# One layer of a streaming encoder on one core: the low parts of a weight panel made by GpSimd in four instructions instead of two

## What is computed

```python
proj = x @ w_in                                   # (T,1024) @ (1024,1792)
q, k = _partial_rotary(q), _partial_rotary(k)     # parts of proj
attn = window attention over chunks of 64         # 8 heads, 2 kv heads, with sinks
c_in = u[..., :512] * sigmoid(u[..., 512:])       # the rest of proj
c = silu(layer_norm(depthwise_conv31(c_in)))
mix = concatenate([attn, c]) @ w_out              # (T,1024) @ (1024,1024)
h = layer_norm(ALPHA * x + mix)
up = depthwise_conv3(h @ w_up)                    # (T,1024) @ (1024,5632)
f = (silu(up[..., :2816]) * up[..., 2816:]) @ w_down
ple = sigmoid(h @ w_pg + b_pg) * (p @ w_pe)
y = layer_norm(ALPHA * h + f + ple)
```

## Time and profile before

| | |
|---|---|
| median of three runs | 2382.76 us (2382.01 to 2384.76) |
| the profiled execution | 2384.01 us, span of its trace 2382.1 us |
| TensorE busy with matmuls | 2347.3 us, 99% |
| VectorE busy | 1423.9 us, 60% |
| ScalarE busy | 1134.5 us, 48% |
| GpSimd busy | 1364.3 us, 57% (1351.5 of it in L545) |
| granted TensorE clock, mean | 0.996 |

### The profile page before, as it was taken

One profiled execution on the slowest core, in us unless ns is written; L12 is line 12 of the kernel. 1 busy time (PEld: TensorE's weight loads), 2 busy tenths in 40 slices (PEclk: granted clock), 3 DMA queues, 4 the chain that ended last, 5 costly groups with the idle time before them and its releaser, 6 DMA issues.

```text
span 2382.1 us, 32873 instructions
## 1 busy us (share of the span) xinstructions
PE 2347.3 (99%) x12705; PEld 2183.0 (92%) x12705; DVE 1423.9 (60%) x2060; ACT 1134.5 (48%) x1859; POOL 1364.3 (57%) x1078
## 2 busy tenths in 40 slices
PE   8999999999999999999999999999999999999997
PEld 8889999999989899999989999999989999999996
DVE  7868777644767665426766765267666553663232
ACT  4446554443555443425554524246535243664452
POOL 7455566576644555557544554676555547676663
PEclk9999999999999999999999999999999999999998
DMA  6333333344333333353433332444333324354432
GB/s 203 111 119 103 125 115 120 118 152 150 108 124 108 104 107 101 115 164 108 136 104 98 106 114 90 143 146 153 98 98 106 114 90 154 118 167 135 143 113 86
DMA packets 99979, 289.77 MB, mean 122 GB/s; under 512 B 13425, under 2 KB 37105, under 8 KB 99825
## 3 DMA queue, kind: packets, MB, share of 16 engines
q1 hardware_dynamic: 82560, 261.77, 35.2%
q10 hardware_dynamic: 17264, 25.91, 3.3%
HBM read 278.74 MB, written 8.99 MB: 121 GB/s over the span
## 4 chain that ended last, share of the span: by engine, by line
PE 95%; DVE 3%; ACT 1%; POOL 0%; DMA 0%; issue 0%; DVEq 0%; ACTq 0%
PE ps L613 31%; PE ps L614 30%; PE ps L615 30%; PE ps L672 1%; PE ps L701 1%; PE ps L692 1%; PE ps L681 1%; DVE turned L1158 1%; DVE sq L1320 0%; DVE res L1257 0%; PE ps L734 0%; DVE turned L1155 0%; DMA a_raw<-in_xT 0%; DVE ps L1157 0%; PE ps L725 0%
## 5 line engine op out<-in xcount | busy, mean ns | idle before, releaser
L545 POOL TENSOR_TENSOR w_lo<-w_raw,w_hi 128x512 fp32r<-128x512 f32 (+2 forms) x1060 | 1351.5, 1300 | 978.3 <-ACT w_hi L772 972.4
L772 ACT CAST w_hi<-w_raw 128x1024 fp32r<-128x1024 f32 (+2 forms) x529 | 516.3, 981 | 552.7 <-PE ps L615 486.8
L613 PE MATMUL ps<-h_hi,w_hi 128*128 128x450 f32 (+5 forms) x2080 | 742.3, 357 | 0.2 <-DVE h_lo L1407 0.2
L614 PE MATMUL ps<-h_lo,w_hi 128*128 128x450 f32 (+5 forms) x2080 | 735.6, 354 | 0.0
L615 PE MATMUL ps<-h_hi,w_lo 128*128 128x450 f32 (+5 forms) x2080 | 734.7, 353 | 0.0
L613 PEld LDWEIGHTS ps<-h_hi,w_hi 128*128 128x128 f32 x2080 | 392.2, 189 | 30.8 <-issue 7.7
L614 PEld LDWEIGHTS ps<-h_lo,w_hi 128*128 128x128 f32 x2080 | 392.2, 189 | 22.1 <-issue 1.5
L615 PEld LDWEIGHTS ps<-h_hi,w_lo 128*128 128x128 f32 x2080 | 391.9, 188 | 21.0
L613 PE MATMUL ps<-f_hi,w_hi 128*128 128x448 f32 (+2 forms) x1072 | 383.1, 357 | 0.0
L614 PE MATMUL ps<-f_lo,w_hi 128*128 128x448 f32 (+2 forms) x1072 | 377.4, 352 | 0.0
L615 PE MATMUL ps<-f_hi,w_lo 128*128 128x448 f32 (+2 forms) x1072 | 377.4, 352 | 0.0
(11 more groups left out here) (153 smaller groups left out, 1935.4 us busy)
## 6 DMA issues: line engine op xcount, KB each, us to landing
w_raw<-in_panels SPq DMA_DIRECT2D x450, 512.0 KB, 3.5
w_raw<-in_panels SPq DMA_DIRECT2D x40, 384.0 KB, 3.0
xres<-in_xT ACTq DMA_DIRECT2D x24, 224.0 KB, 2.7
out_yT<-res ACTq DMA_DIRECT2D x3, 1792.0 KB, 6.2
w_raw<-in_panels SPq DMA_DIRECT2D x40, 128.0 KB, 2.1
a_raw<-in_xT ACTq DMA_DIRECT2D x4, 896.0 KB, 5.9
x_raw<-in_xT SPq DMA_DIRECT2D x2, 896.0 KB, 5.8
a_raw<-in_xT ACTq DMA_DIRECT2D x2, 768.0 KB, 6.3
```

Source lines behind the costliest of these rows:

```text
L545: ins = pool.tensor_tensor(w_lo[:, n % WS, c], w_raw[:, n % RS, c], w_hi[:, n % WS, c].bitcast(F32), ALU.subtract)
L613: pe.matmul(out, w_hi[:, sl, c], hi, start=first, stop=False)
L614: pe.matmul(out, w_hi[:, sl, c], lo, start=False, stop=False)
L772: act.copy(w_hi[:, n % WS, 0:w], w_raw[:, n % RS, 0:w]).then_inc(w_hi_done, 1)
```

## The change

The loop of GpSimd over two halves of a panel becomes a loop over four quarters: 256 columns each for a full panel, 192 for a panel of 768 and 64 for one of 256. What is computed is the same. w_lo_done is signalled behind the fourth quarter. For the first panel, whose cast comes in two halves, the signal first_lo stands behind the second quarter, and the wait for the second half of the cast in front of the third.

```diff
             for n, e in enumerate(ORDER):
                 w = blocks_in(e) * P
                 pool.wait_ge(w_hi_done if n else first_hi, n + 1)
-                for half, c in enumerate((slice(0, w // 2), slice(w // 2, w))):
-                    if n == 0 and half:
+                for quarter in range(4):
+                    c = slice(w // 4 * quarter, w // 4 * quarter + w // 4)
+                    if n == 0 and quarter == 2:
                         pool.wait_ge(w_hi_done, 1)
                     ins = pool.tensor_tensor(w_lo[:, n % WS, c], w_raw[:, n % RS, c], w_hi[:, n % WS, c].bitcast(F32),
                                              ALU.subtract)
-                    if n == 0 and half == 0:
+                    if n == 0 and quarter == 1:
                         ins.then_inc(first_lo, 1)
                 ins.then_inc(w_lo_done, 1)
```

## The result

The changed kernel takes 2386.01 us (median of 20 runs, 2384.66 to 2387.79) against 2382.41 us before (20 runs, 2381.17 to 2385.14): ratio 1.0015, 95% interval 1.0009 to 1.0022. It is 3.6 us slower, clear of the noise but within the 0.2% that the forecast called the same, though it adds 164 us of work to GpSimd: what is gained and what is lost comes from who waits for whom.

The account below looks back on a forecast made before the run. TensorE was taken as the bound, busy 2347.3 of 2382.1 us. Terms -5.6 + 3.0 + 2.6 + 0.9 + 4.0 + 0.4 + 0.4 - 1.6 = +4.1 us on the median 2382.8 gave 2386.9 us, range 2378 to 2393.

Parts of the forecast that it names:

- Price of the cut: GpSimd's w_lo pieces: a quarter takes 0.706 us, a panel 0.32 us more, about 170 us over 530 panels, mostly hidden.
- Part 1, the start: Before the score matmuls near 60 us: VectorE waits less, TensorE's stop shrinks from 4.04 to 0.8 us, clock stays up: -5.6 us.
- Part 2, the boundaries: First panels of new x tiles: additional VectorE turns cost TensorE 3.0, 2.6 and 0.9 us, lower clock 4.0 us.
- (b): Rival: the clock stays up at the two stops near 579 and 1080 us, giving 2382.9 us, no change; chance 0.20.
- Part 3: Small ones: panel at 203.52 us +0.4, two tight pg panels +0.4, shorter waits of trees before two stops -1.6 us.
- (a): Rival: no additional VectorE turns at tile boundaries, quarters run as a block, 0.3 us per panel: 2377.3 us, faster; chance 0.17.
- (c): Rival: the start gains nothing, VectorE's third L1158 stalls 3 to 4 us again, clock falls: 2393 us, slower; chance 0.18.
- at the boundary the one that waits goes next: GpSimd and VectorE block each other for whole instructions; at each boundary the waiting engine gets the next turn.
- VectorE waits for 0.7 us at most: With quarters, VectorE's wait behind a GpSimd piece is at most 0.7 us rather than 1.25.

Follow-up runs that it names:

- e2: Kernel before, with only the first 14 panels of w_lo in quarters, the rest in halves: 2376.77 us against 2382.56.
- e1: Changed kernel, but the first two panels of tiles 2, 3 and 4 in halves again: 2376.37 us against 2382.56 for the kernel before.
- e3: Kernel before, with only the first two panels of tiles 2, 3 and 4 in quarters: 2389.94 us against 2382.56.
- e6: Changed kernel, all quarters kept, with VectorE's tree of squares moved later for tiles 2 to 4: 2378.18 us against 2382.11 for the kernel before.
- e7: Changed kernel with eight pieces per panel instead of four (128 columns for a full panel): 2415.50 us against 2382.11 for the kernel before.
- e11: The kernel with eighths everywhere, unchanged, run once more for one execution: 2425.64 us.
- e10: The kernel with eighths, but halves for panels 0 to 6: 2425.08 us against 2382.85 for the kernel before.
- e9: The changed kernel, unchanged, profiled once more for one execution to see the granted clock: 2386.40 us.

## Why the prediction was right

The forecast was 2386.9 us, the measurement 2386.0. For the profiled execution it was 2388.1, and that took 2385.94: 1.7 of the difference is the clock behind the last stop, which fell in the one profile and not in the other. Part of the closeness is luck: the start gained 0.9 us less in the trace than forecast, the clock at the boundaries cost 0.8 less and the third boundary 0.5 less, and these errors partly cancel. Step by step:

- **Price of the cut.** 0.706 us for a quarter in a row, 0.32 more per panel, 170 us in all. In the changed kernel twelve quarters fill 8.41 us; less the last one's 0.74, they start 0.697 apart, and GpSimd is busy 163.6 us longer. The fixed cost is 0.15 us an instruction. Right, and it was worth 0.3 us only where w_lo was late: new stops of 0.27 us at panels 4 and 7, 0.26 and 0.27 at the two of the pg stage. The other panels kept their cover.
- **Part 1, the start.** Right link by link, at times up to 0.7 us later than forecast. The first multiplication still lost to L554, by 4.25 us; it ended at 39.67 (39.2 forecast). The second L554 started at 51.36 (50.9). The third multiplication took 1.07 us (about 1), the next 1.67, of which 1.1 was waiting (0.8). The scores started at 61.28 (60.6), since TensorE itself came there at 60.36 (59.8). The stop was 0.92 us (0.8), the clock stayed up. The timeline of VectorE in the changed kernel:

```profile
35.42 4.25 DVE L1159 TENSOR_TENSOR turned<-turned,sin 128x384 f32<-128x384 f32 x1
...
50.74 1.07 DVE L1159 TENSOR_TENSOR turned<-turned,sin 128x384 f32<-128x384 f32 x1
...
54.48 1.67 DVE L1159 TENSOR_TENSOR turned<-turned,sin 128x384 f32<-128x384 f32 x1
```

  The sum of -5.6 was -4.7 in that one execution, whose first group started 0.2 us later and was still at the low clock for longer, and -5.8 in e2, timed.
- **Part 2, the boundaries.** Stops of 3.4, 2.6 and about 0.9 us were forecast, of them 3.0, 2.6 and 0.9 new; the stops are 3.42, 2.43 and 0.45, of which 0.52 stood before, and shifts of the groups say 2.9, 2.6 and 0.4. e1 and e3 confirm the place, e6 the cause. The places that the forecast named for the second and third of these panels, 1069 and 1570, left out its own losses ahead of them; with these they are 1074 and 1578, and the trace has 1074.23 and 1577.74. Mis-sized was the clock: 4.0 us for the two, 3.2 in the first profile. And it was too certain: rival (b) had the clock stay up, and over the three executions with these stops it did so at two of six.
- **Part 3.** The panel at 202.9 cost 0.3 us (0.4), two pg panels 0.53 (0.4), the trees -1.7 (-1.6).
- **Rivals.** (a) had no additional turns at the boundaries: excluded by the quarter of 2.52 us. (c) had no gain at the start: excluded. Its opposite mishap, a VectorE operation that stays behind the stream of GpSimd although it waits, was in no rival. The sentence that "at the boundary the one that waits goes next" is the step of the text that the runs refuted, and with it "VectorE waits for 0.7 us at most": true of all waits at halves, of all but one at quarters (about 4.1 us of waiting, at 2007.81), and wrong several times in each execution with eighths, which took 33 to 43 us more than the kernel before, in part for that. The changed kernel was lucky in where its one case fell.

The sum over the changed kernel, from its own rows: -4.7 to the mean at 176, +0.3, +0.5, then +2.9 + 1.5 and +2.6 + 1.7 with small changes between (TensorE's groups are 0.1 nearer or farther here and there), +0.4 and less, -1.7: +3.5 at the last mean, where the medians differ by 3.6.

## What to carry to other kernels

Where GpSimd and VectorE both read two tensors from SBUF, the length of an instruction is also the time for which the other engine may stand, and the number of instructions is the number of turns that it may take: cut the long ones that a critical VectorE chain meets, and leave whole those that TensorE waits for. Both effects can sit in the same edit and hide each other; here +7.4 and -5.8 us by themselves stand beside +3.6 for the whole change, and cutting by place made -8.6. Fine cuts everywhere are no safe course: at 128 columns VectorE sometimes got no turn until GpSimd had nothing left to do.

## What the runs showed of the hardware that I had not expected

- VectorE waiting for GpSimd isn't always served at the next boundary: 15.4 us (e7), 14.7 us (e11) and 19.2 us (e10) for a multiplication that lasts 0.55, always while GpSimd ran short pieces back to back, some with an L554 among them.
- The granted clock behind the same stop differs between executions of the same stop: behind 3.42 us it fell in two of three (0.74 of full over 6.6 us, 0.55 over 6.8), behind 2.43 us in two of three, and behind the last stop of 1.81 us it fell in 5 of the 12 profiles (before, e6, e7, e9, e10) and in the others not before TensorE had finished. So the falls are a matter of the execution as well as of the length of the stop, and a difference of some 2 us between two single executions can be this alone.
